# Delta rule on one core: the transpose of X from VectorE's block transposes, two weight pieces moved behind X

## The chip, the cores and the metric

The kernel runs on one core of a Trainium2 chip. The metric is the device time of one execution in microseconds. A core has TensorE (PE in the rows; PEld is its load of the stationary operand), VectorE (DVE), ScalarE (ACT), GpSimd (POOL) and SyncE (SP), each with its own instruction stream, in order; they wait for each other by semaphores.

## The reference

Two stacked blocks of layers on 512 tokens of width 1024: pool, gated delta rule, latent attention, pool, then a state-space and convolution layer and a differential attention layer. The change touches the gated delta rule alone. It has 8 heads (keys of 128, values of 256) and chunks of 64 tokens. For each head and chunk:

```
g = cumsum(g); decay = exp(where(causal, g_i - g_j, -inf))
L = where(strict, (k_beta @ k.T) * decay, 0)
A = eye(64) + L
sol = triangular_solve(A, [v_beta, k_beta * exp(g)], lower=True)
attn = where(causal, (q @ k.T) * decay, 0)
# scan over chunks: v_new = u - w @ state; o = q*exp(g) @ state + attn @ v_new; state is updated
o = rmsnorm(o) * silu(gate); out = o @ w_out
```

q, k and v come from a projection of h, a causal convolution of 4 taps along the tokens and a silu.

## The kernel before, in words

All float32 products with weights are made of three products in fp32r: high part by high, high by low, low by high (lines 334 to 336). A weight slot of 128x1024 is copied from `raw` by ScalarE to its high part (`whi`, line 296, "hi") and GpSimd subtracts to get the low part (`wlo`, line 311, four instructions of 128x256 a slot). A **piece** is one k step of one tile: three matmuls of 512 columns. There are four slots and four banks for such tiles.

The delta rule's function is `gdn_layer`. For each head the inverse of A is made by doubling: P2, P4, P8 are powers of the strictly triangular part within 16x16 blocks (`Pw`) and V is the sum; then X is the part above these blocks, and X2, X2V widen the inverse from 16 to 64; "join" and "joined" combine two chunks of 64 into one of 128. Each is `four(...)`, 4 products over the four column groups (8 matmuls in the rows, line 1939). Where a product is to be multiplied from the left, its transpose is needed as the stationary operand. For P2, P4, P8, V8 and X2 the helper `turn` on VectorE makes it from 32x32 block transposes (line 2156), one instruction for all four groups of one block, and writes it into a buffer `left[...]` that was set to zero once. For X there is another way: TensorE makes the transpose by a second product (`four(2, left[2], left[0], "X turned")`), for which ScalarE lays out `left[2]` (two copies, line 2102), and ScalarE copies the result from PSUM to `left[3]` (line 2113). VectorE copies X itself to `Pw` (line 2241).

Between the steps of the inverse, TensorE makes weight pieces for the same head's V1 (values' second half), the next head's K, Q, V0, the gate tiles z and output tiles. `SITES` names the places behind each product, `EARLY` and `PIECES` say how many pieces are made at each (`more(site)`); all that are left come at the end of the head. Head 0 also makes 6 pieces of head 1 (`AHEAD`). On VectorE the generator `behind_vector` yields, in a fixed order, the tile's multiplication out of its bank ("take", line 1869), 4 convolution taps (line 1881 for tap 0, line 1884 for taps 1 to 3) for V1, K, Q and V0 in turn, the takes of z (line 1874) and the residual additions (line 606); `TAKES` and `TAKES_BETWEEN` (heads 1 to 6) say how many of these steps are done at each site (`fill(site)`). ScalarE follows with silu of a tile after its tap 3 (line 1913). TensorE's transposes of the values (`v_tokens`, line 1957) wait for that silu of V1:

```
more("X2V")
pe.wait_ge(*ae.of(f"{i} silu {V1}"))
pe.wait_ge(*ve.of(f"{i} A"))
v_tokens(0)
pe.wait_ge(*ve.of(f"{i} U"))
```

On VectorE, `U` (line 2255, two additions) comes after the wait for X2V, and `fill("U")` after it. Between `X` and `X2` VectorE also makes the low parts of the previous head's y (`y_before(2)`, `y_before(3)`, line 2315).

Of the kernel before, what the change touches and what calls it, by code (L numbers as in the profile page):

```python
# [24 lines left out]
P = 128  # L25
# [11 lines left out]
NCH = SEQ // P  # L37
# [105 lines left out]
class Steps:  # L143
# [20 lines left out]
    def at(self, name, i=0, ago=0):  # L164

        per = self.counts.get("per turn", 1)
        return self.sem, self.counts.get(name, 1) + (i - ago + 1) * per


def program(nc, T, out, counts, layers):  # L170
# [5 lines left out]
    ACT = mybir.ActivationFunctionType  # L176
# [16 lines left out]
    with top:  # L193
        area = [top]

        def sb(name, shape, dt=F32):
            return area[0].enter_context(nc.sbuf_tensor(name, shape, dt))
# [12 lines left out]
        def steps(section, *engines):  # L210
            return [Steps(sem(f"{section}_{e}"), counts.setdefault((section, e), {})) for e in engines]
# [21 lines left out]
        def wbank(b):  # L233
            return psum[:, BANKS + b, :]
# [63 lines left out]
        def hi_after(act, sec, i, j, last):  # L298

            for nxt in W.ahead(sec, i, j, last):  # L300
                slot_hi(act, *nxt)
# [490 lines left out]
        def even_layer(n, l):  # L792

            S = f"even{n}"
            GROUPS, HG, H, TAPS, EARLY = 4, 4, 16, 31, 15
            PADU = TAPS - 1
# [209 lines left out]
            def first_taps(act, c):  # L1006
# [4 lines left out]
                if c > 1:  # L1011
                    act.wait_ge(*ve.of(f"tap {c - 2} {EARLY - 1}" if odd else f"conv {c - 2}"))
                act.activation(at(0), src[:, 0:SEQ], ACT.Identity, scale=dw[:, 32 * c:32 * c + 1],  # L1013
# [5 lines left out]
            def tap(dve, c, k):  # L1019

                odd = c % 2
                src, at = taps_of(c)
                if k < 2 - odd:
                    return
                before = k - 1 if odd else k - 2
                dve.wait_ge(*(ae if before < 2 - odd else ve).of(f"tap {c} {before}"))
                out, old = at(k), at(k)
                if k >= (EARLY - 1 if odd else TAPS - 1):
                    out = conv31[:, c, :]
                if odd and k >= EARLY:  # L1030
                    old = conv31[:, c, :]
                dve.scalar_tensor_tensor(out=out, in0=src[:, k:k + SEQ], scalar=dw[:, 32 * c + k:32 * c + k + 1], in1=old,  # L1032
                                         op0=ALU.mult, op1=ALU.add).then_inc(*ve.done(f"tap {c} {k}"))

            def late_taps(dve, q0, q1):

                for q in range(q0, q1):
                    a, k = 1 + 4 * (q // (TAPS - EARLY)), EARLY + q % (TAPS - EARLY)
                    tap(dve, a, k)
                    tap(dve, a + 2, k)  # L1040

            def glu_vector(dve, t, other):
                a, b = 2 * t, 2 * t + 1
                take_u(dve, a)
                if t:
                    tap(dve, b - 2, EARLY - 2)
                    tap(dve, b - 2, EARLY - 1)
# [604 lines left out]
        def gdn_layer(n, l):  # L1652
# [3 lines left out]
            H, DV, BA = 8, 256, 0  # L1656
# [13 lines left out]
            U = sb("U", [P, NCH, P])  # L1670
            Nt = sb("g_Nt", [P, NCH, 64])
            PU = sb("g_PU", [P, NCH, P])
            left = [sb(f"g_left{x}", [P, NCH, P]) for x in range(5)]
            Pw, V = PU[:, :, 0:64], PU[:, :, 64:P]
            Ghl = sb("Ghl", [P, SEQ], F32R)
            pick = sb("g_pick", [P, H], F32R)
# [9 lines left out]
            in16, above, one64 = (masks[:, 3 * P + x * 64:3 * P + (x + 1) * 64] for x in range(3))  # L1686
            Y, Dinv = d1, d2
# [9 lines left out]
            ae, te, ve = steps(S, "scalar", "tensor", "vector")  # L1697
            x_ready_before = x_ready[-1][-1]
            K, QQ, V0, V1 = 1, 0, 2, 3
            LO, HI = slice(0, 64), slice(64, P)  # L1700
# [28 lines left out]
            def chunks(ap):  # L1729
                return ap.rearrange("p (c n) -> p c n", c=NCH)  # L1730
# [7 lines left out]
            def half(b):  # L1738
                return wbank(b)[:, 0:NCH * 64].rearrange("p (c n) -> p c n", c=NCH)

            def rows(g):
                return slice(32 * g, 32 * g + 32)

            def cols(g):
                return slice(32 * (g % 2), 32 * (g % 2) + 32)
# [8 lines left out]
            def gate_vector(dve):  # L1754
# [51 lines left out]
                dve.tensor_tensor(r, wbank(0)[:, 96:128], gcol[:, 1, :, :].rearrange("p c h -> p (c h)"), ALU.subtract)\  # L1806
                   .then_inc(*ve.done("last-G"))
                yield
                for t0 in (U, Nt, left[0], left[1], left[2], left[4]):
                    dve.memset(t0[:, :, :], 0.0).then_inc(*ve.done("zeros " + t0.name))  # L1810
                dve.wait_ge(*te.of("G rows"))
                dve.tensor_copy(Ghl[0:8, :], wbank(0)[0:8, :]).then_inc(*ve.done("rows hi"))
# [120 lines left out]
            def work_tensor(pe, i, more):  # L1933
# [3 lines left out]
                def four(b, left, right, name, n=P):  # L1937
                    for c in range(NCH):
                        last = pe.matmul(wbank(b)[:, c * n:(c + 1) * n], left[:, c, :], right[:, c, :],  # L1939
                                         start=True, stop=True)  # L1940
                    last.then_inc(*te.done(f"{i} {name}"))
# [45 lines left out]
                four(2, left[1], V, "PV8", 64)  # L1987
                more("PV8")
                pe.wait_ge(*ve.of(f"{i} V8 turned"))
                pe.wait_ge(*ae.of(f"{i} above blocks"))  # L1990
                four(2, left[2], left[0], "X turned")
                four(0, left[0], Nt, "X", 64)
                more("X")
                pe.wait_ge(*ve.of(f"{i} X"))
                pe.wait_ge(*ae.of(f"{i} X turned"))
                four(1, left[3], PU, "X2")
                more("X2")
                pe.wait_ge(*ve.of(f"{i} V32"))
                four(2, left[4], V, "X2V", 64)
                more("X2V")  # L2000
                pe.wait_ge(*ae.of(f"{i} silu {V1}"))
                pe.wait_ge(*ve.of(f"{i} A"))
# [12 lines left out]
                for c in range(NCH):  # L2015
# [20 lines left out]
                    for d in range(2):  # L2036
                        last = pe.matmul(wbank(2 + d)[:, c * P:(c + 1) * P], vn[:, c % 2, d * P:(d + 1) * P],
                                         A[:, c, :], start=c == 0, stop=True)
# [24 lines left out]
            def work_scalar(act, i, rest_before):  # L2063
# [18 lines left out]
                for g in range(4):  # L2082
                    last = act.activation(left[0][rows(g), :, rows(g)], N[rows(g), :, rows(g)], ACT.Copy)
# [13 lines left out]
                for j in rest_before:  # L2097
                    hi_after(act, S, 0, j, True)
                hi_after(act, S, 0, hi[0], True)
                act.wait_ge(*ve.of(f"{i} above"))  # L2100
                for part in (LO, HI):
                    last = act.activation(left[2][part, :, part], Nt[part], ACT.Copy)
                last.then_inc(*ae.done(f"{i} above blocks"))
                if i:
                    y_hi(act, i - 1, 0)
                else:
# [2 lines left out]
                if i:  # L2109
                    y_hi(act, i - 1, 1)  # L2110
                hi_after(act, S, 0, hi[1], True)
                act.wait_ge(*te.of(f"{i} X turned"))
                act.activation(left[3][:, :, :], chunks(wbank(2)), ACT.Copy).then_inc(*ae.done(f"{i} X turned"))
                hi_after(act, S, 0, hi[2], True)
                silu(act, V1, i)
                if i:
# [36 lines left out]
            def turn(dve, i, name, src, dst, spread_out, blocks):  # L2153
                for at_row, at_col in blocks:
                    to = dst[rows(at_col), :, rows(at_row) if spread_out else cols(at_row)]
                    last = dve.transpose(to, src(at_row, at_col))  # L2156
                last.then_inc(*ve.done(f"{i} {name} turned"))

            def add_to_v(dve, i, more, before, name):
                dve.wait_ge(*ve.of(f"{i} {before}"))  # L2160
                dve.tensor_tensor(V, V, more, ALU.add).then_inc(*ve.done(f"{i} {name}"))  # L2161

            def work_vector(dve, i, fill, y_before):
# [74 lines left out]
                dve.tensor_tensor(eg[:, :], stream(QQ, i), eg[:, :], ALU.mult).then_inc(*ve.done(f"{i} q exp G"))  # L2238
                fill("V8")
                dve.wait_ge(*te.of(f"{i} X"))  # L2240
                dve.tensor_copy(Pw, half(0)).then_inc(*ve.done(f"{i} X"))
                if i:
                    y_before(2)
                    y_before(3)
                fill("X")
                dve.wait_ge(*te.of(f"{i} X2"))
                turn(dve, i, "X2", lambda to, of: chunks(wbank(1))[rows(to), :, cols(of)], left[4], True, [(0, 1), (2, 3)])
                add_to_v(dve, i, chunks(wbank(1))[:, :, 64:P], "V8", "V32")
                dve.wait_ge(*ae.of(f"{i} 1/norm k"))
                dve.tensor_tensor(cV, rk, beta, ALU.mult).then_inc(*ve.done(f"{i} beta/norm"))  # L2250
# [54 lines left out]
            def y_vector(dve, i, part):  # L2305
# [6 lines left out]
                else:  # L2312
# [4 lines left out]

            SITES = ["kk", "P2", "P4", "P8", "PV8", "X", "X2", "X2V", "join", "joined", "v new 0", "o 0", "kS 1", "v new 1",
                     "o 1", "kS 2", "v new 2", "o 2", "kS 3", "v new 3", "o 3"]
            EARLY = [8, 3, 3, 3, 3, 2, 2, 2, 3, 3]  # L2320
            PIECES = {i: EARLY + [2] * 6 + [1] * 4 + [5] for i in (1, 2, 3, 4)}
            AHEAD = 6
            PIECES[0] = EARLY + [2] * 6 + [1] * 4 + [AHEAD]
# [3 lines left out]
            TAKES = {0: {"P2": 2, "V2": 2, "A": 1, "V8": 2, "X": 2, "V32": 3, "U": 1, "Y": 1, "U joined": 1,  # L2327
                         "v new 0": 2, "state 0": 2, "rhs 1": 2, "v new 1": 2, "state 1": 1, "rhs 2": 1, "v new 2": 1,
                         "v new 3": 1},
                     H - 1: {"V2": 1, "V8": 1, "X": 1, "V32": 2, "U": 1, "U joined": 1,  # L2330
                             "v new 0": 1, "state 0": 1, "rhs 1": 1, "v new 1": 1, "state 1": 1,
                             "rhs 2": 1, "v new 2": 1, "state 2": 1, "rhs 3": 1, "v new 3": 2, "o summed": 2}}
            TAKES_BETWEEN = {"V2": 1, "V8": 1, "X": 1, "V32": 2, "U": 1, "Y": 1,
                             "U joined": 1, "v new 0": 2, "state 0": 2, "rhs 1": 2, "v new 1": 2,
                             "state 1": 2, "rhs 2": 2, "v new 2": 1, "v new 3": 1, "o summed": 2}

# [57 lines left out]
            def vector(dve):  # L2394
# [13 lines left out]
                for i in range(H):  # L2408
                    taking = behind_vector(dve, i)
                    takes = TAKES.get(i, TAKES_BETWEEN)  # L2410

# [590 lines left out]
        def odd_layer(n, l):  # L3002
# [595 lines left out]
            def gpsimd(pool):  # L3598
# [6 lines left out]
            return merge(nv, me)  # L3605

        STAGE = {"load": load_x, "pool": pool_layer, "gdn": gdn_layer, "mla": mla_layer, "even": even_layer,
                 "odd": odd_layer, "store": store_x}

# [334 lines left out]
```

## Time and profile before

| | us |
|---|---|
| median of 3 runs | 2474.79 (2472.77 to 2477.22) |
| the profiled execution, its own time | 2474.79 |
| its span | 2473.0 |
| delta rule's 8 heads, about | 345 to 848 of the span |

The page gives for each engine the busy time, share of the span and number of instructions. Times in the rows are microseconds from the start of the span; a row of a timeline has the start, the length, the engine, line and operation, what is written from what, the count of merged instructions, and in brackets how long the engine was idle before and who ended that.

### The profile page before, as it was taken

The numbers are of one execution on the slowest core, as the hardware profiler recorded it, in microseconds if no ns is written. First come the engines' busy times: TensorE is split into PE (matmuls) and PEld (weight loads), VectorE is DVE, ScalarE is ACT, GpSimd is POOL, SyncE is SP. The second block draws the span as 40 slices with busy tenths as digits, with TensorE's granted clock in tenths as the row PEclk, the third lists the DMA queues.
The fourth block names the chain that finished last, engine by engine and source line by source line (L and its number), as shares of the span: only waits on it lengthen the run. The fifth ranks groups of instructions, "written<-read, shape, count | busy, mean of one in ns | idle before, by whom it ended". The sixth has DMA issues, their size and how long they took to land.

```text
span 2473.0 us, 31476 instructions
## 1 busy us (share of the span) xinstructions
PE 2435.5 (98%) x11606; PEld 1950.2 (79%) x11606; DVE 1649.3 (67%) x2898; ACT 1034.5 (42%) x1697; POOL 1191.4 (48%) x1447
## 2 busy tenths in 40 slices
PE   9999999999999999999999999999999999999999
PEld 7888877788888787777777788888888777867777
DVE  7644687777777665434343656546998998477776
ACT  4222254444444354333333332224544668454443
POOL 7665643333343375334443366666554534644342
PEclk9999999999999999999999999999999999999999
DMA  4233221121111132222222132233322211321211
GB/s 161 86 103 111 94 82 53 59 63 66 60 61 51 53 129 86 67 79 73 80 77 79 60 103 94 87 104 101 102 94 85 72 53 52 122 77 60 69 60 43
DMA packets 60008, 198.43 MB, mean 80 GB/s; under 512 B 7248, under 2 KB 9936, under 8 KB 59856
## 3 DMA queue, kind: packets, MB, share of 16 engines
q1 hardware_dynamic: 56976, 192.90, 23.8%
q10 hardware_dynamic: 2880, 3.51, 0.6%
q8 instruction: 94, 1.54, 0.3%
q14 instruction: 58, 0.48, 0.1%
HBM read 191.93 MB, written 2.10 MB: 78 GB/s over the span
## 4 chain that ended last, share of the span: by engine, by line
PE 86%; DVE 10%; ACT 2%; issue 1%; DMA 0%; SPq 0%; ACTq 0%; DVEq 0%
PE psum L334 23%; PE psum L336 23%; PE psum L335 22%; PE psum L1939 3%; PE psum L2842 1%; PE psum L2827 1%; DVE psum L1032 1%; PE psum L2845 1%; PE psum L3303 1%; DVE e_c L1032 1%; DVE e_stg L1202 1%; PE psum L3280 1%; PE psum L2818 1%; DVE g_left L2156 1%; PE psum L2027 1%
## 5 line engine op out<-in xcount | busy, mean ns | idle before, releaser
L311 POOL TENSOR_TENSOR wlo<-raw,whi 128x256 fp32r<-128x256 f32 x1436 | 1190.9, 862 | 1255.2 <-ACT whi L296 1255.1
L334 PE MATMUL psum<-xh,whi 128*128 128x512 f32 x1800 | 732.9, 407 | 1.4 <-DVE e_stg L1202 1.4
L336 PE MATMUL psum<-xh,wlo 128*128 128x512 f32 x1800 | 705.0, 392 | 0.0
L335 PE MATMUL psum<-xl,whi 128*128 128x512 f32 x1800 | 703.7, 391 | 0.0
L296 ACT ACTIVATE whi<-raw 128x1024 fp32r<-128x1024 f32 (+1 forms) x369 | 378.4, 1031 | 723.3 <-PE psum L336 698.5
L336 PEld LDWEIGHTS psum<-xh,wlo 128*128 128x128 f32 x1800 | 339.1, 188 | 73.7
L334 PEld LDWEIGHTS psum<-xh,whi 128*128 128x128 f32 x1800 | 340.0, 189 | 72.2 <-issue 6.7
L335 PEld LDWEIGHTS psum<-xl,whi 128*128 128x128 f32 x1800 | 339.8, 189 | 67.3 <-issue 2.9
L606 DVE TENSOR_TENSOR xT<-psum,xT 128x512 f32<-128x512 f32 x232 | 155.4, 686 | 161.7 <-PE psum L336 153.7
L702 DVE TENSOR_TENSOR pool_u<-psum,R 128x512 f32<-128x512 f32 x32 | 21.9, 691 | 122.8 <-PE psum L336 122.7
L334 PE MATMUL psum<-pool_y,whi 128*128 128x512 f32 x256 | 99.6, 389 | 0.0
L335 PE MATMUL psum<-pool_y,whi 128*128 128x512 f32 x256 | 99.6, 389 | 0.0
L336 PE MATMUL psum<-pool_y,wlo 128*128 128x512 f32 x256 | 99.6, 389 | 0.0
L1032 DVE SCALAR_TENSOR_TENSOR psum<-e_ue,par,psum 128x512 f32<-128x512 f32 x112 | 79.7, 747 | 3.4 <-ACT psum L1013 3.4
L2782 DVE TENSOR_TENSOR mwork<-psum,R 128x512 f32<-128x512 f32 x16 | 11.1, 691 | 86.0 <-PE psum L336 86.0
L2871 ACT ACTIVATE mwork<-psum,nmx 128x128 f32<-128x128 f32 (+3 forms) x64 | 33.7, 528 | 82.3 <-DVE nmx L2935 82.2
L2933 DVE TENSOR_REDUCE mxs<-psum 128x1 f32<-128x128 f32 (+3 forms) x64 | 31.1, 487 | 51.6 <-PE psum L2847 51.6
L1884 DVE SCALAR_TENSOR_TENSOR g_qv<-pre,par,g_qv 128x512 f32<-128x512 f32 x72 | 62.0, 861 | 1.1
L1939 PEld LDWEIGHTS psum<-g_PU,g_left 128*128 128x128 f32 x384 | 48.4, 193 | 14.6 <-DVE g_PU L2161 6.0
L334 PE MATMUL psum<-gy,whi 128*128 128x512 f32 x128 | 56.2, 439 | 2.3 <-issue 1.2
L334 PE MATMUL psum<-cq,whi 128*128 128x512 f32 x144 | 58.1, 404 | 0.0
L1939 PE MATMUL psum<-g_PU,g_left 128*128 128x64 f32 (+1 forms) x384 | 52.1, 279 | 4.4 <-DVE g_PU L2161 2.2
(563 smaller groups left out, 4345.6 us busy)
## 6 DMA issues: line engine op xcount, KB each, us to landing
raw<-weights_dram SPq DMA_DIRECT2D x329, 512.0 KB, 3.6
raw<-weights_dram SPq DMA_DIRECT2D x40, 384.0 KB, 3.0
xin<-x_dram SPq DMA_DIRECT2D x4, 512.0 KB, 6.2
mla_xrot<-sq ACTq DMA_DIRECT2D x32, 64.0 KB, 2.0
out_dram<-xT SPq DMA_DIRECT2D x8, 256.0 KB, 2.1
par<-params_dram SPq DMA_DIRECT2D x1, 323.5 KB, 8.3
g_masks<-gdn_masks_dram ACTq DMA_DIRECT2D x1, 288.0 KB, 2.8
mwork<-positions_dram ACTq DMA_DIRECT2D x1, 256.0 KB, 3.6
```

The costliest lines, as they stand in the source:

```text
L296: act.activation(whi[:, q, 0:nk * nm * P], raw[:, q, 0:nk * nm * P], ACT.Copy).then_inc(hi_ready[q], 1)
L311: last = pool.tensor_tensor(wlo[:, q, part], raw[:, q, part], whi[:, q, part].bitcast(F32), ALU.subtract)
L334: pe.matmul(gbank(b), whi[:, q, c:c + P], h, start=k == 0, stop=False)
L335: pe.matmul(gbank(b), whi[:, q, c:c + P], l, start=False, stop=False)
L336: done = pe.matmul(gbank(b), wlo[:, q, c:c + P], h, start=False, stop=k == nk - 1)
L606: dve.tensor_tensor(xT[:, t, :], tile(sec, j, m), xT[:, t, :], ALU.add).then_inc(*taken(sec, j, m))
L1032: dve.scalar_tensor_tensor(out=out, in0=src[:, k:k + SEQ], scalar=dw[:, 32 * c + k:32 * c + k + 1], in1=old, op0=ALU.mult, op1=ALU.add).th ...
L1202: op = dve.scalar_tensor_tensor(out=stg[:, g % 2, x, s:], in0=bank(j)[:, 0:SEQ - s], scalar=conv[:, 20 * g + 5 * x + k:20 * g + 5 * x + k ...
L1884: dve.scalar_tensor_tensor(out=dst, in0=pre[:, x, k:k + SEQ], scalar=w, in1=dst, op0=ALU.mult, op1=ALU.add).then_inc(*ve.done(f"{i} tap {k ...
L1939: last = pe.matmul(wbank(b)[:, c * n:(c + 1) * n], left[:, c, :], right[:, c, :], start=True, stop=True)
L2871: act.activation(prob[:, hd, off_q[t]:off_q[t] + w], wbank(x % 4)[:, 0:w], ACT.Exp, scale=SCALE, bias=nmx[:, x:x + 1], accum_out=rs[:, x:x ...
L2933: dve.reduce_max(mxs[:, x:x + 1], wbank(x % 4)[:, 0:w], AX.X).then_inc(*ve.done(f"{i} max raw {x}"))
```

## The change

X's transpose is made by `turn` on VectorE from the PSUM bank in which TensorE left X: six block transposes into `left[2]`, ahead of the copy of X to `Pw`. TensorE's second product, ScalarE's two copies ahead of it and ScalarE's copy behind it go, and the wait for them; one of the five `left` buffers goes, and the others are renumbered. In `EARLY`, two pieces more are made behind X, one less behind join and one less behind joined. In `TAKES_BETWEEN` and in the last head's `TAKES` the one step at X goes; heads 1 to 6 get it back at Y, the last head at U. Head 0's `TAKES` stay.

```diff
-            left = [sb(f"g_left{x}", [P, NCH, P]) for x in range(5)]
+            left = [sb(f"g_left{x}", [P, NCH, P]) for x in range(4)]
...
                 pe.wait_ge(*ve.of(f"{i} V8 turned"))
-                pe.wait_ge(*ae.of(f"{i} above blocks"))
-                four(2, left[2], left[0], "X turned")
                 four(0, left[0], Nt, "X", 64)
                 more("X")
                 pe.wait_ge(*ve.of(f"{i} X"))
-                pe.wait_ge(*ae.of(f"{i} X turned"))
-                four(1, left[3], PU, "X2")
+                four(1, left[2], PU, "X2")
                 more("X2")
                 pe.wait_ge(*ve.of(f"{i} V32"))
-                four(2, left[4], V, "X2V", 64)
+                four(2, left[3], V, "X2V", 64)
...
-                act.wait_ge(*ve.of(f"{i} above"))
-                for part in (LO, HI):
-                    last = act.activation(left[2][part, :, part], Nt[part], ACT.Copy)
-                last.then_inc(*ae.done(f"{i} above blocks"))
...
-                act.wait_ge(*te.of(f"{i} X turned"))
-                act.activation(left[3][:, :, :], chunks(wbank(2)), ACT.Copy).then_inc(*ae.done(f"{i} X turned"))
                 hi_after(act, S, 0, hi[2], True)
...
                 dve.wait_ge(*te.of(f"{i} X"))
+                turn(dve, i, "X", lambda to, of: half(0)[rows(to), :, cols(of)], left[2], True,
+                     [(0, 0), (1, 1), (2, 2), (3, 3), (0, 1), (2, 3)])
                 dve.tensor_copy(Pw, half(0)).then_inc(*ve.done(f"{i} X"))
...
-            EARLY = [8, 3, 3, 3, 3, 2, 2, 2, 3, 3]
+            EARLY = [8, 3, 3, 3, 3, 4, 2, 2, 2, 2]
...
-                     H - 1: {"V2": 1, "V8": 1, "X": 1, "V32": 2, "U": 1, "U joined": 1,
+                     H - 1: {"V2": 1, "V8": 1, "V32": 2, "U": 2, "U joined": 1,
...
-            TAKES_BETWEEN = {"V2": 1, "V8": 1, "X": 1, "V32": 2, "U": 1, "Y": 1,
+            TAKES_BETWEEN = {"V2": 1, "V8": 1, "V32": 2, "U": 1, "Y": 2,
```

## Rows read from the trace of the kernel before

**Rows 1.** The page's first part: engines, busy us, share of the span, instructions.

```profile
span 2473.0 us, 31476 instructions
...
PE 2435.5 (98%) x11606; PEld 1950.2 (79%) x11606; DVE 1649.3 (67%) x2898; ACT 1034.5 (42%) x1697; POOL 1191.4 (48%) x1447
```

**Rows 2.** Waits of TensorE, 345 to 860 us: total, times, longest.

```profile
PE psum L1939 <- ACT g_qv L1913: 2.5, 1, 2.5
PE psum L1939 <- DVE g_PU L2161: 2.2, 6, 0.8
```

**Rows 3.** TensorE's timeline in head 4, from X turned to join's pieces.

```profile
614.64 1.05 PE L1939 MATMUL psum<-g_left 128*128 128x128 f32 x8
615.52 1.00 PE L1939 MATMUL psum<-g_Nt,g_left 128*128 128x64 f32 x8
616.34 0.47 PE L334 MATMUL psum<-xh,whi 128*128 128x512 f32 x1
...
617.11 0.40 PE L334 MATMUL psum<-xh,whi 128*128 128x512 f32 x1
...
617.80 1.05 PE L1939 MATMUL psum<-g_PU,g_left 128*128 128x128 f32 x8
618.61 0.48 PE L334 MATMUL psum<-xh,whi 128*128 128x512 f32 x1
...
620.07 1.07 PE L1939 MATMUL psum<-g_PU,g_left 128*128 128x64 f32 x8
620.95 0.48 PE L334 MATMUL psum<-xh,whi 128*128 128x512 f32 x1
...
622.43 0.60 PE L1957 MATMUL psum<-cst,g_qv 128*128 128x128 f32 x4
622.96 0.67 PE L1950 MATMUL psum<-U,N 64*64 64x64 f32 x8
```

**Rows 4.** VectorE's timeline in head 4, from V2's turn to U's fill.

```profile
606.28 1.29 DVE L2156 STREAM_TRANSPOSE g_left<-psum 32x128 f32<-32x128 f32 x4 [1.03 <-PE psum L1939]
...
615.54 0.47 DVE L1881 TENSOR_SCALAR g_qv<-pre,par 128x512 f32<-128x512 f32 x1
616.57 0.43 DVE L2241 COPY g_PU<-psum 128x256 f32<-128x256 f32 x1 [0.55 <-PE psum L1939]
616.91 1.28 DVE L2315 TENSOR_TENSOR gy<-vb,gy 128x512 fp32r<-128x512 f32 x2
618.11 0.75 DVE L1884 SCALAR_TENSOR_TENSOR g_qv<-pre,par,g_qv 128x512 f32<-128x512 f32 x1
618.89 0.64 DVE L2156 STREAM_TRANSPOSE g_left<-psum 32x128 f32<-32x128 f32 x2
619.56 0.42 DVE L2161 TENSOR_TENSOR g_PU<-g_PU,psum 128x256 f32<-128x256 f32 x1
...
619.98 1.53 DVE L1884 SCALAR_TENSOR_TENSOR g_qv<-pre,par,g_qv 128x512 f32<-128x512 f32 x2
621.54 0.87 DVE L2255 TENSOR_TENSOR U<-g_PU,psum 64x256 f32<-64x256 f32 x2
622.34 0.68 DVE L1869 TENSOR_TENSOR pre<-psum,R 128x512 f32<-128x512 f32 x1
```

**Rows 5.** ScalarE's timeline in head 4.

```profile
620.33 1.06 ACT L296 ACTIVATE whi<-raw 128x1024 fp32r<-128x1024 f32 x1 [4.01 <-PE psum L336]
621.55 0.64 ACT L1913 ACTIVATE g_qv<-g_qv 128x512 f32<-128x512 f32 x1 [0.16 <-DVE g_qv L1884]
```

**Rows 6.** GpSimd's timeline, one slot's low parts in head 4.

```profile
621.47 2.81 POOL L311 TENSOR_TENSOR wlo<-raw,whi 128x256 fp32r<-128x256 f32 x4 [6.39 <-ACT whi L296]
```

**Rows 7.** Two taps of K beside GpSimd's low parts in head 4.

```profile
630.37 2.40 DVE L1884 SCALAR_TENSOR_TENSOR g_k<-pre,par,g_k 128x512 f32<-128x512 f32 x2
...
630.36 3.71 POOL L311 TENSOR_TENSOR wlo<-raw,whi 128x256 fp32r<-128x256 f32 x4 [6.08 <-ACT whi L296]
```

**Rows 8.** Windows on TensorE: start:end, length, busy (instructions), clock, DMA.

```profile
417.50:421.00 3.50, 2.03 (x18) 1.00 0.00 0
2189.00:2192.50 3.50, 1.54 (x11) 1.00 0.44 150
```

**Rows 9.** TensorE's timeline behind that second window.

```profile
2191.04 0.49 PE L3303 MATMUL psum<-o_kn,o_qr 64*128 64x128 f32 x4 [1.96 <-DVE o_kn L3172]
...
2193.04 0.63 PE L336 MATMUL psum<-xh,wlo 128*128 128x512 f32 x1
2193.47 0.63 PE L334 MATMUL psum<-xh,whi 128*128 128x512 f32 x1
```

**Rows 10.** Head 7: a gate tile's take on VectorE, the piece that waits on TensorE.

```profile
819.95 0.67 DVE L1874 TENSOR_TENSOR gs<-psum,R 128x512 f32<-128x512 f32 x1
...
818.89 0.68 PE L1950 MATMUL psum<-d 64*64 64x64 f32 x8
819.50 0.50 PE L334 MATMUL psum<-gy,whi 128*128 128x512 f32 x1
...
820.67 0.50 PE L334 MATMUL psum<-gy,whi 128*128 128x512 f32 x1 [0.20 <-DVE gs L1874]
```

More of the change, by code:

```diff
@@ L1808, in gate_vector @@
                 yield
-                for t0 in (U, Nt, left[0], left[1], left[2], left[4]):
+                for t0 in (U, Nt, left[0], left[1], left[2], left[3]):
                     dve.memset(t0[:, :, :], 0.0).then_inc(*ve.done("zeros " + t0.name))
@@ L2246, in work_vector @@
                 dve.wait_ge(*te.of(f"{i} X2"))
-                turn(dve, i, "X2", lambda to, of: chunks(wbank(1))[rows(to), :, cols(of)], left[4], True, [(0, 1), (2, 3)])
+                turn(dve, i, "X2", lambda to, of: chunks(wbank(1))[rows(to), :, cols(of)], left[3], True, [(0, 1), (2, 3)])
                 add_to_v(dve, i, chunks(wbank(1))[:, :, 64:P], "V8", "V32")
```

## The prediction

> **What bounds the kernel now.** I read the page first: TensorE is busy for 2435.5 of 2473.0 us, the next engine for 1649.3 [rows 1]. A microsecond taken from TensorE is a microsecond of the kernel, unless TensorE then waits. The waits of TensorE in the delta rule come next: a single one of 2.5 us is the largest, and six on the inverse's additions make 2.2 us together [rows 2]. So its 8 heads hold almost no waiting, and what matters is how near each hand-over is to being late. For that I read the three timelines of head 4, which is like heads 2, 3, 5 and 6 to within 0.1 us in most places. TensorE goes from product to pieces to product with no idle time in brackets [rows 3]. VectorE has none either from X's copy at 616.57 to U's end at 622.41 [rows 4]: in this stretch it is as full as TensorE, though its share of the span is only 67%. ScalarE's silu of V1 starts at 621.55, 0.04 after VectorE's last tap of V1 (619.98 + 1.53), and is over at 622.19; TensorE takes it up at 622.43 [rows 3 to 5]. That hand-over has 0.24 us to spare, and it is the one to watch.
>
> **What the change takes away.** "X turned" goes from TensorE: 614.64 to 615.52, 0.88 us a head [rows 3], 7.0 us over 8 heads. ScalarE loses three copies a head that nobody waits for in head 4; that is worth nothing on the path. It has a side effect: ScalarE no longer stops for X turned, but in head 4 it stopped 4.01 us more for a slot's last piece anyway [rows 5].
>
> **What it adds between X and X2.** Four block transposes from PSUM take 1.29 us, two take 0.64 [rows 4], so six take 1.94 and X's copy 0.43 behind them. Head 4, step by step: X starts at 614.64, its pieces at 615.50 (0.86 later). VectorE is free at 616.01, so the turn runs 616.05 to 617.99 and the copy to 618.44. Two pieces last from 616.34 to 617.80, 1.46 us, one more 0.695 (three of 0.232; 617.11 is the fourth matmul) [rows 3], so four end at 618.36. X2 starts at about 618.49: a stall of 0.13 us. The two added pieces do cover the turn, with nothing left over.
>
> **What it does to V1's taps.** This decides. The steps on VectorE are taken from a fixed order: V1's take, taps 0, 1, 2, 3, then K's take. Before, V2 and V8 took the first two, X tap 1, V32 taps 2 and 3, U K's take (618.11, 619.98 and 622.34) [rows 4]. Without X's step, V32 gets taps 1 and 2, and tap 3 falls to U: behind the wait for X2V and both additions of U. TensorE waits for V1's silu ahead of all that. In head 4: X's copy starts at 618.01, the two low parts of y end their turn at 619.55 (1.54 after the copy's start, as 616.57 to 618.11). X2's pieces start at 619.30 and its result is there at about 619.53. Turn of X2 and addition take 1.09 (618.89 to 619.98): V32 at 620.67. X2's two pieces end at 620.76, X2V follows without a stall, its pieces start at 621.64 (0.88 on) and end at 623.12. On VectorE: taps 1 and 2 until 622.21, U's additions, tap 3 from 623.04 to 623.79, silu of 0.64 until 624.47, transposes of the values at 624.60. TensorE stands from 623.12. It has made 28 pieces instead of 26 by then, so the old 622.43 compares with 623.82 (2 x 0.695 more): **0.78 us late**, the 0.88 us already deducted. The later sites give up the two pieces, and the sequence from the transposes on has the old lengths; the copies behind join and joined still fit under two pieces (1.46 us against 0.42 each and their latency). Nothing at the end of a head gives the time back, since there VectorE waits for TensorE and not the other way.
>
> **The same with GpSimd beside it.** The slot of Q is free once its last piece is made. That piece moves from behind X2 to behind X: the end of these sites goes from 620.07 to 618.36, ScalarE's high part from 620.33 to 618.6, GpSimd's four low parts from 621.47 [rows 5, 6] to about 619.8. There they lie on taps 1 and 2, which ran free of them at 619.98. Two taps beside GpSimd's low parts took 2.40 us [rows 7] against 1.53 alone [rows 4]: 0.87 more. Then the head is 0.78 + 0.87 = **1.65 us late**. Bounds are 0.78 (no contact) and 1.65 (full); I take 1.65, since four low parts last 2.8 to 3.7 us and both taps fit inside.
>
> The Trainium skill speaks against the change at this place (GPSIMD Engine Reference, section 8, Key points): GpSimd shares its SBUF interfaces with VectorE and contends with VectorE instructions that have two SBUF inputs. A tap has two, and 2.40 against 1.53 us agrees; by that rule the taps are slowed wherever the low parts fall, without it each of these heads would lose 0.78.
>
> **The other heads.** Head 6 has an earlier VectorE by 0.16 us at the X2 turn: 1.5. Head 1 is 6 pieces ahead, its high part comes much earlier and its taps, slow before, run free: 0.2 gained (from there to 0.8 lost). Head 0 keeps its takes, but VectorE is full there: the turn starts late, both X2 and X2V wait some 0.8 us, and 0.6 us is lost on net at join (0.3 to 1.2). Head 7 is like head 6 up to the transposes, 1.5. There one more thing is late: the piece of "joined" that needs z's bank. It waited for the take that ends at 820.62 and started at 820.67, 1.17 behind the first piece at 819.50 [rows 10]. With one piece more made ahead of joined, it is now the first one there, and the 1.17 stands empty: the stretch keeps its length and makes a piece less, up to 0.7 lost; I take 0.6. Sum of stalls, the saving deducted: 0.6 - 0.2 + 4 x 1.65 + 1.5 + 2.1 = **10.6 us**. With no contact between taps and low parts: 0.6 - 0.2 + 4 x 0.78 + 0.6 + 1.2 = 5.3 us.
>
> **The clock.** TensorE's idle time ahead of the values' transposes grows from nothing to about 1.3 us (no contact) or 2.2 (full). After idle of 1.96 us at 2191.04 its granted clock, 2.4 GHz, fell to 1.2: matmuls go from 0.39 to 0.63 us, a start every 0.43 instead of 0.23 us [rows 9]. The windows' clock is 1.00 up to 2192.5, the fall comes right behind [rows 8]. After idle of 1.5 us around 418 with 2.03 us busy of 3.5 it stayed at 1.00 [rows 8]. So six heads (2 to 7) may each fall or not. Eight matmuls at 0.43 cost 8 x 0.20 = 1.6 us, my price for one fall, by the length of the slow stretch in the rows. I count one fall for the forecast, 1.6 us, and leave none and six as bounds.
>
> Forecast: 2474.8 + 10.6 + 1.6 = 2487.0, **2487 us**. The profiled execution's own time is 2474.79, which is also the median of the three runs; its span is 1.8 us less.
>
> **Rivals.**
> (a) Late, but without contact: the low parts miss the taps. Then +5.3 and no fall: 2480. For it: some taps beside low parts took only 0.74. Against it: the high part hangs on a piece that comes 1.7 us earlier.
> (b) The wait for V1's silu doesn't bind, and U alone sets join. U ends at 622.24 + 0.87 = 623.11 in head 4, the transposes 0.53 behind 623.12: join is not held, so heads 2 to 7 save 0.7 each (623.65 with 28 pieces against 622.96 with 26, 1.39 apart), head 1 0.2, and head 0 loses 0.6: -3.8, 2471. It would need tap 3 to be done by about 622.4 (0.64 of silu and 0.1 ahead of 623.12); the order of steps puts it at 623.8 at the earliest. Little speaks for it.
> (c) Faster in full: the removed product's 0.88 us counts in all heads because ScalarE, relieved of three copies, and the later pieces hide everything: -7.0, 2468. It decides from the same point, tap 3's end before 622.4, and needs VectorE idle somewhere between 616 and 622.4; the rows show none.
> (d) Worse: a fall of the clock in each of six heads: 2474.8 + 10.6 + 9.6 = 2495. For it: 2.2 us idle is more than 1.96, and light work (values' transposes, join) follows. Against it: dense pieces on both sides.
>
> **How the numbers follow.** Forecast with none to three falls, 2482 to 2491: 0.58. (a) 0.20, half of it inside 0.2%. (b) 0.06. (c) 0.06. (d) 0.10. 0.2%, 5 us, is about what a measurement of this kernel tells from no change. Slower: 0.58 + 0.10 + 0.10 = 0.78. Same: 0.10 + 0.06 = 0.16. Faster: 0.06. The range for 8 in 10 is 2477 to 2495: it holds the forecast, (a) and most of (d) up to its edge.
>
> **What would show it.** In the changed kernel's heads 2 to 6: TensorE's values' transposes with idle time of 1.3 to 2.2 us, ended by ScalarE's silu (line 1913 before), some 9 to 13 us over 7 heads in the waits. VectorE: tap 3 of V1 as a single tap behind U's additions. X2 waiting for X's copy by 0.1 to 0.2 us, about 0.8 in head 0. Two taps ahead of U at 2.4 us rather than 1.53, GpSimd beside them. The turn of X at 1.94 us for six. A granted clock under 1.00 in some heads. It is wrong if the silu's wait is not there, if X2's wait is over 0.5 us in the middle heads (then the turn is dearer than rows of other turns say), or if a head's period does not grow.

## The result and the profile after

The changed kernel takes 2502.35 us (median of 4 runs, 2499.01 to 2509.76) against 2475.15 of the kernel before: a ratio of 1.0117 (95% interval 1.0105 to 1.0129), so 27 us slower. The forecast was slower, 2487 us, in a range of 2477 to 2495. The way and the place were right, the size was not.

The waits of TensorE in the delta rule come first (total, times, longest), the answer to [rows 2]:

```profile
PE psum L1957 <- ACT g_qv L1913: 15.9, 7, 2.7
PE psum L1939 <- DVE g_PU L2152: 2.7, 7, 1.1
```

A wait that had been 0.2 us once is now 15.9 us in seven heads: the values' transposes wait for ScalarE's silu of V1. Head 4 on TensorE, answering to [rows 3] (this head runs 9.05 us later than before):

```profile
623.69 1.01 PE L1939 MATMUL psum<-g_Nt,g_left 128*128 128x64 f32 x8
624.51 0.48 PE L334 MATMUL psum<-xh,whi 128*128 128x512 f32 x1
...
627.42 1.16 PE L1939 MATMUL psum<-g_PU,g_left 128*128 128x128 f32 x8
...
629.81 1.06 PE L1939 MATMUL psum<-g_PU,g_left 128*128 128x64 f32 x8
...
631.91 0.40 PE L336 MATMUL psum<-xh,wlo 128*128 128x512 f32 x1
634.84 0.66 PE L1957 MATMUL psum<-cst,g_qv 128*128 128x128 f32 x4 [2.53 <-ACT g_qv L1913]
```

The same head on VectorE, answering to [rows 4]:

```profile
624.98 1.93 DVE L2147 STREAM_TRANSPOSE g_left<-psum 32x128 f32<-32x128 f32 x6
626.94 0.43 DVE L2234 COPY g_PU<-psum 128x256 f32<-128x256 f32 x1
...
629.28 0.42 DVE L2152 TENSOR_TENSOR g_PU<-g_PU,psum 128x256 f32<-128x256 f32 x1
629.62 0.58 DVE L2243 TENSOR_TENSOR g_small<-g_small,gcol 128x4 f32<-128x4 f32 x1
630.13 2.43 DVE L1884 SCALAR_TENSOR_TENSOR g_qv<-pre,par,g_qv 128x512 f32<-128x512 f32 x2
632.59 0.87 DVE L2248 TENSOR_TENSOR U<-g_PU,psum 64x256 f32<-64x256 f32 x2
633.39 0.74 DVE L1884 SCALAR_TENSOR_TENSOR g_qv<-pre,par,g_qv 128x512 f32<-128x512 f32 x1
```

And ScalarE, then GpSimd in it, answering to [rows 5, 6]:

```profile
627.62 1.06 ACT L296 ACTIVATE whi<-raw 128x1024 fp32r<-128x1024 f32 x1 [6.40 <-PE psum L336]
634.16 0.63 ACT L1913 ACTIVATE g_qv<-g_qv 128x512 f32<-128x512 f32 x1 [5.48 <-DVE g_qv L1884]
```

```profile
628.76 3.26 POOL L311 TENSOR_TENSOR wlo<-raw,whi 128x256 fp32r<-128x256 f32 x4 [4.64 <-ACT whi L296]
```

This is the whole chain: the slot's last piece comes earlier, its high part starts at 627.62, the low parts from 628.76 lie on two taps (2.43 us against 1.53 before), tap 3 stands alone behind U, the silu follows right behind it, and TensorE is idle for 2.53 us.

What the waits do not show is in the windows by clock (start:end, length, busy time and count of PE, PEld, DVE, ACT and POOL, granted clock as a share of 2.4 GHz, DMA share and GB/s):

```profile
504.20:514.40 10.20, 10.20 (x39) 7.86 (x40) 2.70 (x6) 2.99 (x6) 0.64 (x1) 0.50 0.00 0
572.50:575.80 3.30, 3.30 (x14) 2.25 (x13) 1.00 (x2) 0.22 (x1) 0.00 (x0) 0.50 0.00 0
698.80:702.10 3.30, 3.30 (x11) 2.09 (x10) 1.43 (x3) 0.59 (x2) 0.00 (x0) 0.50 0.00 0
767.10:773.80 6.70, 6.54 (x30) 4.78 (x30) 1.50 (x3) 1.32 (x4) 0.00 (x0) 0.50 0.01 4
838.70:848.90 10.20, 9.09 (x37) 6.77 (x35) 1.43 (x3) 2.09 (x5) 0.00 (x0) 0.50 0.02 6
603.70:666.30 62.60, 59.88 (x324) 48.88 (x323) 50.53 (x101) 25.83 (x50) 23.92 (x28) 1.00 0.19 59
```

Behind the idle time of heads 2, 3, 5, 6 and 7 the clock is at 0.50, 1.2 GHz, for 34 us in all; head 4 (last row) is spared. The kernel before had two such falls in these heads, 3.4 us each, behind a wait of 2.46 us in head 0 and behind waits of 0.63 and 1.39 us at the start of head 2:

```profile
358.32 1.16 PE L1939 MATMUL psum<-g_qv,g_k 128*128 128x128 f32 x8 [2.46 <-ACT g_qv L1913]
472.06 0.70 PE L1963 MATMUL psum<-Ghl,g_pick 128*128 128x512 f32 x1 [1.39 <-DVE vb L2293]
```

```profile
359.00:363.00 4.00, 4.00 (x19) 3.52 (x18) 1.99 (x7) 2.51 (x5) 3.71 (x6) 0.57 0.02 4
472.00:476.00 4.00, 3.94 (x14) 3.51 (x15) 3.86 (x10) 3.96 (x6) 0.00 (x0) 0.57 0.00 0
```

The changed kernel has the same waits there (2.48 us, 0.61 and 1.39) and no fall. The time from one head's first product (line 1963) to the next one's, in us, from the timelines:

| head | 0 | 1 | 2 | 3 | 4 | 5 | 6 |
|---|---|---|---|---|---|---|---|
| before | 64.6 | 61.4 | 62.0 | 60.5 | 60.5 | 65.9 | 66.3 |
| of it at 1.2 GHz | 3.4 | 0 | 3.4 | 0 | 0 | 0 | 0 |
| after | 64.0 | 61.8 | 67.3 | 64.1 | 62.6 | 69.5 | 71.2 |
| of it at 1.2 GHz | 0 | 0 | 10.2 | 3.4 | 0 | 3.4 | 6.8 |
| e1 (busy in the idle time) | 64.0 | 65.3 | 62.7 | 62.6 | 62.6 | 68.0 | 68.4 |
| of it at 1.2 GHz | 0 | 6.8 | 0 | 0 | 0 | 0 | 0 |
| e9 (the best) | 63.7 | 60.1 | 59.8 | 59.7 | 59.5 | 65.1 | 65.7 |
| of it at 1.2 GHz | 3.4 | 0 | 0 | 0 | 0 | 0 | 0 |

Heads 0 to 6 lose 19.1 us, head 7 and all behind it 6.6, what lies ahead of head 0 0.5; the span grew by 26.1.

### The profile page after: what moved, and what is told of

The parts are those of the page before. It is cut to its first block, busy times and chain, and to the rows that moved or that the text cites. A ratio compares the mean times of both kernels' runs of the same rounds, so it can differ in the third digit from the quotient of the medians.

```text
span 2499.1 us, 31356 instructions
## 1 busy us (share of the span) xinstructions
PE 2444.7 (98%) x11542; PEld 1951.7 (78%) x11542; DVE 1668.8 (67%) x2946; ACT 1023.8 (41%) x1673; POOL 1193.2 (48%) x1447
## 4 chain that ended last, share of the span: by engine, by line
PE 84%; DVE 11%; ACT 3%; issue 2%; DMA 0%; SPq 0%; ACTq 0%; DVEq 0%
PE psum L334 23%; PE psum L336 22%; PE psum L335 22%; PE psum L1939 2%; PE psum L2835 1%; PE psum L2820 1%; DVE psum L1032 1%; DVE g_qv L1884 1%; PE psum L2838 1%; PE psum L3296 1%; DVE e_c L1032 1%; DVE g_left L2147 1%; DVE e_stg L1202 1%; PE psum L3273 1%; PE psum L2811 1%
## 5 line engine op out<-in xcount | busy, mean ns | idle before, releaser
L1884 DVE SCALAR_TENSOR_TENSOR g_qv<-pre,par,g_qv 128x512 f32<-128x512 f32 x72 | 67.4, 936 | 1.1
```

The source lines that it names most:

```text
L1884: dve.scalar_tensor_tensor(out=dst, in0=pre[:, x, k:k + SEQ], scalar=w, in1=dst, op0=ALU.mult, op1=ALU.add).then_inc(*ve.done(f"{i} tap {k ...
```

## The experiments

The theory was: (1) V1's tap 3 behind U makes TensorE wait for the silu; (2) the low parts of Q's slot, earlier by two pieces, lie on the taps and add to it; (3) the idle time lets the clock fall, which costs about as much again. The rival was that the six block transposes cost what is lost. Each run is compared with the kernel before on the same chip (medians 2473.5 to 2474.4 us).

**e1, TensorE kept busy in the idle time** (on the changed kernel):

```diff
                 more("X2V")
-                pe.wait_ge(*ae.of(f"{i} silu {V1}"))
                 pe.wait_ge(*ve.of(f"{i} A"))
+                if i:
+                    for _ in range(8):
+                        pe.matmul(wbank(3), pick[:, i:i + 1].to_broadcast([P, P]), Ghl[:, :], start=True, stop=True)
+                pe.wait_ge(*ae.of(f"{i} silu {V1}"))
                 v_tokens(0)
```

> The changed kernel with eight extra products of 512 columns (1.85 us together) on TensorE ahead of its wait for V1's silu in heads 1 to 7; their result is overwritten by the values' transposes. They stand inside the 2.4 us in which TensorE waits anyway, so the stall's end does not move. Theory 'stall and clock' (some 12 us of stalls, 15 us of the clock at 1.2 GHz for 34 us behind them): the clock stays at 1.00 from 480 to 850 us, and the time falls by 12 to 16 us, to 2487 to 2490. Rival 'stall alone' (the clock's fall costs little because others catch up): no change, 2500 to 2504.

2490.14 us, 1.0067 (1.0052 to 1.0082). Eight useless products made the kernel 12.2 us faster than the changed kernel. TensorE's timeline in head 4, and its window over heads 2 to 7, with the changed kernel's window behind:

```profile
629.81 2.00 PE L2001 MATMUL psum<-Ghl,g_pick 128*128 128x512 f32 x8
632.45 0.65 PE L1957 MATMUL psum<-cst,g_qv 128*128 128x128 f32 x4 [0.64 <-ACT g_qv L1913]
```

```profile
475.00:865.00 390.00, 379.60 (x2022) 309.55 (x2023) 303.08 (x604) 154.58 (x283) 143.04 (x172) 1.00 0.17 56
```

```profile
475.00:860.00 385.00, 365.39 (x1891) 296.64 (x1890) 289.78 (x581) 146.51 (x273) 137.14 (x164) 0.96 0.17 55
```

The products and the rest of the wait last 2.64 us, where the wait alone lasted 2.53, and head 4, in which the changed kernel's clock stayed up, lasts 62.6 us in both. So the products do nothing but keep the clock, and its falls are worth 12 us. In the profiled executions the time from the start of head 2 to the end fell by 14.1 us. Head 1 gave 3.5 back: there this run has a fall of its own, 6.8 us long, behind a wait of 2.15 us at which the changed kernel waits as long and keeps its clock.

```profile
419.70 1.62 PE L1939 MATMUL psum<-g_PU,g_left 128*128 128x64 f32 x7 [2.15 <-ACT g_left L2083]
```

```profile
419.60:426.80 7.20, 7.10 (x25) 6.35 (x26) 3.84 (x10) 3.67 (x5) 2.84 (x4) 0.53 0.22 72
```

What is left is 15.8 us over the kernel before. The mean granted clock of the two profiled executions is the same, 0.997, so this is stalls: heads 3 and 4 have 62.6 against 60.5, 2.1 each.

**e2, tap 3 ahead of U** (on the changed kernel): `"V32": 3` and one step less at `"U"`, heads 1 to 7.

> The changed kernel with V1's tap 3 at V32 (three steps there, one less at U), so ahead of the wait for X2V and of U's additions. Theory 'V1's tap 3 behind U is what TensorE waits for': the silu comes about 0.8 us earlier, the idle time ahead of the values' transposes goes from 2.5 to 1.7 us, 6 to 7 heads, and fewer falls of the clock: 2482 to 2492. Rival 'the six block transposes ahead of X2 are what costs': nothing gained, 2499 to 2504.

2492.05 us (2483.23 to 2493.07), 1.0063. The wait for the silu went from 15.9 to 10.5 us, 1.6 to 1.7 in a head, as expected. The clock still fell behind three of these six waits, 6.8 us each time. The executions of this kernel lie 10 us apart, those of the changed kernel 10.8, and the granted clock goes with them: the one of 2483.23 us had a mean clock of 0.997, the other three of 2491 to 2493 us 0.992 and 0.993; the changed kernel had 0.992 at 2499.01 and 0.986 at 2509.76. How often the clock falls is thus not the same from one execution of a kernel to the next, and a trace shows one of them.

**e3, VectorE's steps alone** (on the kernel before): only the two tables of `TAKES` as changed.

```diff
-            TAKES_BETWEEN = {"V2": 1, "V8": 1, "X": 1, "V32": 2, "U": 1, "Y": 1,
+            TAKES_BETWEEN = {"V2": 1, "V8": 1, "V32": 2, "U": 1, "Y": 2,
```

> The kernel before with the changed kernel's steps on VectorE alone (X's step goes, to Y or U); X's transpose stays on TensorE, the pieces stay. Theory 'tap 3 behind U': idle of some 1.8 us ahead of the values' transposes in heads 2 to 7, +10 us, and falls of the clock on top: 2486 to 2500. Rival 'the transposes cost': within 2 us of the kernel before.

2486.26 us, 1.0049 (1.0034 to 1.0064). X's transpose is still on TensorE, and 12 us are lost. The wait ahead of the values' transposes is 1.2 us in heads 2 to 7 and not 1.8 as expected, and none of these six was followed by a fall in the profiled execution; 1.73 us in head 1 was. Head 4:

```profile
627.12 0.40 PE L336 MATMUL psum<-xh,wlo 128*128 128x512 f32 x1
628.72 0.66 PE L1957 MATMUL psum<-cst,g_qv 128*128 128x128 f32 x4 [1.20 <-ACT g_qv L1913]
```

**e4, the steps as before** (on the changed kernel), the counterpart:

> The changed kernel with the steps on VectorE as before (tap 1 at X, taps 2 and 3 at V32). Theory 'tap 3 behind U': the idle time splits, 1.3 us ahead of X2V and about 0.5 ahead of the values' transposes, each head loses about 1 us against before, no or few falls of the clock: 2479 to 2484. Rival 'the transposes cost': 2495 or more, with the wait ahead of X2 or X2V of 2 us and more.

2477.27 us, 1.0016 (1.0007 to 1.0025), better than expected. With the transposes on VectorE and the pieces moved, but the old steps, 25 of the 27 us are gone. The idle time is split, 0.43 ahead of X2V (1.3 was expected) and 0.65 ahead of the values' transposes, and in the profiled execution the clock never fell in heads 0 to 7. Head 4:

```profile
620.41 1.10 PE L1939 MATMUL psum<-g_PU,g_left 128*128 128x64 f32 x8 [0.43 <-DVE g_PU L2152]
623.62 0.66 PE L1957 MATMUL psum<-cst,g_qv 128*128 128x128 f32 x4 [0.65 <-ACT g_qv L1913]
```

e3 and e4 together put the cause at the steps, and refute the rival. The transposes are not free even so: a middle head of e4 lasts 61.4 us against 60.5 before, though TensorE has 0.88 less to do.

**e6, the transposes alone** (on the kernel before): `turn` in place of the product, steps and pieces as before.

> The kernel before with only X's transpose moved to VectorE: pieces and steps as before. Theory 'the two pieces cover the turn': TensorE waits ahead of X2 for 1.4 us in every head and 0.5 to 0.7 in all behind; each head loses about 1.4 us against before: 2481 to 2487, falls of the clock few. Rival 'the two moved pieces are themselves harmful through GpSimd's low parts on the taps': no worse than with them (2477.3).

2484.96 us, 1.0046 (1.0031 to 1.0061). The waits:

```profile
PE psum L1939 <- DVE g_PU L2234: 10.7, 8, 2.0
PE psum L1939 <- DVE g_PU L2152: 4.3, 12, 0.6
```

The first is X2 waiting for X's copy behind the turn: 1.3 us in a middle head. With the two pieces there (e4) it is gone but for 0.6 us in head 0, and 7.7 us between the medians with it. The two pieces did what they are for.

**e7, GpSimd still while the taps run** (on the changed kernel):

```diff
-                hi_after(act, S, 0, hi[2], True)
                 silu(act, V1, i)
...
                 act.activation(Dinv[LO, :, LO], quarter(2), ACT.Copy).then_inc(*ae.done(f"{i} U turned"))
+                hi_after(act, S, 0, hi[2], True)
```

> The changed kernel with ScalarE's high part of the slot of Q (and with it GpSimd's four low parts) moved behind the copy of U turned, so that GpSimd is still while VectorE makes V1's taps. Theory 'contact with GpSimd costs 1.3 us a head': taps 1 and 2 back to 1.53 us, the small product to 0.16, idle ahead of the values' transposes 1.2 to 1.4 us instead of 2.5, and with it no or few falls of the clock: 2480 to 2487. Rival 'contact is not it': 2499 to 2504, idle unchanged.

2482.71 us, 1.0036 (1.0024 to 1.0047): 20 us less than the changed kernel, by moving one ScalarE copy. VectorE in head 4:

```profile
621.55 0.16 DVE L2243 TENSOR_TENSOR g_small<-g_small,gcol 128x4 f32<-128x4 f32 x1
621.63 1.53 DVE L1884 SCALAR_TENSOR_TENSOR g_qv<-pre,par,g_qv 128x512 f32<-128x512 f32 x2
```

0.16 and 1.53 us stand where 0.58 and 2.43 were, and the idle time of TensorE is 1.20. A head lasts 61.3 us, 1.3 less than with contact at the same clock (62.6 in e1). In the profiled execution the clock stayed up in heads 2 to 6 and fell in head 7, for 13.6 us, and at the start of head 1, for 3.4.

**e5, V1's steps where VectorE has room** (on the changed kernel):

```diff
-            TAKES_BETWEEN = {"V2": 1, "V8": 1, "V32": 2, "U": 1, "Y": 2,
+            TAKES_BETWEEN = {"P2": 1, "V2": 1, "A": 1, "V8": 1, "V32": 1, "U": 1, "Y": 1,
```

and in the last head the same, with a gate tile's take at U and at Y.

> The changed kernel with V1's steps where VectorE has room: take at P2 (idle 1.0 us there), tap 0 at V2, tap 1 at A (idle 0.6), tap 2 at V8, tap 3 at V32; in the last head the two gate takes at U and Y. Theory 'tap 3 behind U and a full VectorE from X to U': the silu comes ahead of need, idle ahead of the values' transposes under 0.3 us, ahead of X2 and X2V 0.3 to 0.5, and TensorE's saved 0.88 us a head shows: 2468 to 2473, faster than the kernel before. Rival 'the transposes on VectorE can't be covered': X2 or X2V wait over 1 us a head, 2478 or more.

2470.84 us, 0.9990 (0.9981 to 1.0000), an interval that just reaches no change. The silu is no longer waited for; 0.35 us ahead of X2 is left in each middle head, since tap 2 at V8 delays the turn.

**e8, e5 with e7's edit**, measured twice:

> Both of the two before: V1's steps early and the low parts of Q's slot late. If both mechanisms are as said, it is the fastest: tap 3 at V32 without contact, TensorE without idle over 0.5 us: 2466 to 2471. If the late high part makes a weight slot late, idle shows ahead of pieces instead (2475 or more).

2469.86 us, 0.9987 (0.9978 to 0.9997), and again:

> The kernel of e8 once more in five rounds, beside e9 on the same chip: 2468 to 2472, faster than the kernel before by 0.1 to 0.2%.

2470.54 us, 0.9989 (0.9980 to 0.9998). Against e5 that is no difference that the intervals tell.

**e9, e8 with tap 2 at V32** instead of V8:

> As e8, with V1's tap 2 at V32 behind the addition and not at V8 ahead of the turn of X (heads 1 to 7). If what is left of idle in e8 (0.35 us ahead of X2 in each of heads 2 to 6) comes from tap 2 standing ahead of the turn, it goes, the silu gets 0.7 us later and just binds (0 to 0.3 us), and each head gains up to 0.3 us: 2467 to 2471. If the silu binds by more than 0.4 us, nothing is gained: 2470 to 2472.

2467.36 us, 0.9975 (0.9965 to 0.9985): faster than the kernel before by 6.1 us. Its median is 3.2 below that of e8 beside it, but the two intervals overlap a little. TensorE in head 4, around X2 and the values' transposes:

```profile
612.78 0.40 PE L336 MATMUL psum<-xh,wlo 128*128 128x512 f32 x1
613.01 1.05 PE L1939 MATMUL psum<-g_PU,g_left 128*128 128x128 f32 x8
...
617.41 0.40 PE L336 MATMUL psum<-xh,wlo 128*128 128x512 f32 x1
617.64 0.60 PE L1957 MATMUL psum<-cst,g_qv 128*128 128x128 f32 x4
```

No idle time of that kind is left there. Heads 3 and 4 last 59.7 and 59.5 us against 60.5 before, 0.8 and 1.0 less, which agrees with the 0.88 us of the product that was taken away, and against 60.2 in e8. That is 0.5 to 0.7 a head over e8 where up to 0.3 was expected; where the rest comes from stays open.

## Why the prediction was right and wrong

**What bounds it, and where it would be late: right.** The hand-over with 0.24 us to spare was the one that broke. Steps taken from a fixed order had pushed V1's tap 3 behind U; e3 shows that this alone is enough.

**The added transposes: right.** Six took 1.93 us (forecast 1.94), X2 started 627.42 - 9.05 = 618.37 (618.49), X2V 620.76 (620.76). Head 0 waited 0.6 and 0.5 us there, not 0.8 twice. It came out 0.65 us shorter than before where I had 0.6 lost, but that is luck with the clock: the kernel before had its fall in head 0 and the changed kernel had none. In e2 and e5, which leave head 0 as changed and had that fall, it lasted 64.71 and 64.96 us against 64.64, so 0.1 and 0.3 lost.

**Contact with GpSimd: right in kind, a third too small.** The taps took 2.43 (2.40), but the product on 128x4 ahead of them, which has two inputs in SBUF too, went from 0.16 to 0.58, and I had counted only the taps. The transposes of the values came at 625.79 on the old clock against a forecast of 625.47: 2.0 us late and not 1.65. In all, stalls cost 15.8 us (e1), not 10.6. Heads 3 to 6 have 2.0 to 2.1 each where I had 1.65 and 1.5, head 7 with all behind it 2.9 where I had 2.1, and head 1 lost 0.4 where I had a gain of 0.2: its first product from the left waits 2.15 us for ScalarE (1.47 before), and its values' transposes 1.2. Heads 0 and 2 can't be compared so, since the kernel before has a fall of the clock in each.

**The clock: this is the step that failed.** I counted one fall and priced it at "8 x 0.20 = 1.6 us". Five came, with stretches of 3.4, 3.4, 6.8, 10.2 and 10.2 us at 1.2 GHz. For a stretch of 3.4 us the price was right: heads 3 and 5 last 1.4 to 1.5 us more than in e1. It was taken for every fall, and the longer ones cost 2.8 us (6.8 us, head 6), 4.6 (10.2 us, head 2) and 3.7 (10.2 us, head 7 with all behind it). So the clock's term was 14 us in these heads and 12.2 between the medians (e1), against 1.6; it is over 10 of the 15 us by which the forecast missed, and the stalls are the rest. Rival (d), six falls at 1.6 us, was held to be the far end; with it the sum is 2495, still 7 short.

The number of falls could have been put higher. The idle time itself, 2.2 us, was read rightly (2.0 to 2.7), and [rows 8] and [rows 9] had a fall behind 1.96 us and none behind 1.5, so all six heads stood beyond the larger one; the two falls in heads 0 and 2 of the kernel before were not counted at all. The forecast should have been 10.6 + 6 falls, with room in the range for longer ones. But a wait's length alone does not say whether the clock falls: in head 4 it stayed up behind 2.53 us, and in head 0 it fell behind 2.46 us before and stayed up behind 2.48 us after.

The rule of the Trainium skill (GPSIMD Engine Reference, section 8) that GpSimd contends with VectorE instructions that have two SBUF inputs held: e7 takes the contact away and the two durations return. In the kernel before, four block transposes from PSUM took 1.28 to 1.29 us and U's additions, which read PSUM, 0.87 us, beside GpSimd and without it. (The turn of X in the rows above ran while GpSimd was idle.) Two SBUF inputs are not the only case, though: tap 0 has one tensor input and took 0.93 to 1.04 us beside GpSimd, against 0.47 without it, in head 0 of the kernel before.

What stays open: why the clock falls behind a wait in one execution and not behind the same wait in another, and why a stretch at 1.2 GHz lasts 3.4 us in one head and 10.2 in another. At 504.2 TensorE was busy for all of 10.20 us, so idle time within it was not what kept the clock down.

## What to carry to other kernels

When work goes from one engine to another, follow every instruction that is queued behind it in order, and ask who waits for those: here the transposes were covered, and a convolution tap pushed two sites back by a table of steps cost the time. Where TensorE would stand for more than a microsecond again and again, price the clock before the stall, by trying it with useless products in the gap. An engine's busy share of 67% says nothing of a stretch of 6 us in which it is full.

## What the runs showed of the hardware

Waits of TensorE ahead of the values' transposes in heads 2 to 7, and how many were followed by a fall of the granted clock to 1.2 GHz, each in one profiled execution: 0.65 us, none of 6 (e4); 1.2 us, none of 6 (e3) and one of 6 (e7, head 7, where two more waits of 1.1 us follow); 1.6 to 1.75 us, three of 6 (e2); 2.0 to 2.7 us, five of 6 (the changed kernel). Behind a gap filled with products, none of 6 (e1).

The same wait in the same place can go either way. Ten traces (the changed kernel, e1, e2 and e4 to e9, e8 twice) have 2.14 to 2.17 us at the first product from the left of head 1; the clock fell behind it in five (e1, e2, e7, e8 twice) and stayed up in five.

Beside GpSimd's subtractions one VectorE tap of 128x512 with both tensor inputs in SBUF grows by some 0.45 us (1.53 to 2.43 us for two), and a product on 128x4 by nearly as much, 0.16 to 0.58 us.
